# Cached attention on one core: two neighbouring tokens of a page on each partition, so that a page load is 64 rows of 6 KB and 2 KB instead of 128 rows of 3 KB and 1 KB

## The reference, cut to what matters

```python
past_len = page_table.shape[1] * PAGE_SIZE          # 16 pages x 128 tokens
g = pool[page_table]                                # pages of one sequence, in order
# mixer B, stick-breaking, 6 heads x 64, k and v of a token: 2 x 6 x 64 floats = 3 KB
z = einsum('bqhd,bkhd->bhqk', q, k) * HEAD_DIM ** -0.5
after = cumsum(log_keep, reverse=True) - log_keep
a = exp(log_sigmoid(z) + after);   y = einsum('bhqk,bkhd->bqhd', a, v)
# mixer C, sparse, 6 query heads over 2 kv heads x 64, k and v of a token: 1 KB
logits = q . k  + (0 or out of reach, from the indexer's top 256);   softmax;   y = p . v
```

## Time and profile before

| | |
|---|---|
| median of 3 runs | 4626.3 us (4622.88 to 4626.41) |
| the profiled execution | 4624.24 us, span 4622.5 us |
| mean granted TensorE clock | 0.97 |
| busy share of the span | PE 92%, PEld 52%, DVE 75%, ACT 38%, POOL 23% |
| cached attention, layer 0 | from the first page load of its own at 1833.2 us to the issue of the output stage's first load at 2053.6 us |
| cached attention, layer 1 | from 4139.8 us to 4360.4 us |

### The profile page before, as it was taken

One profiled execution on the slowest core, in us unless ns is written; L12 is line 12 of the kernel. 1 busy time (PEld: TensorE's weight loads), 2 busy tenths in 40 slices (PEclk: granted clock), 3 DMA queues, 4 the chain that ended last, 5 costly groups with the idle time before them and its releaser, 6 DMA issues.

```text
span 4622.5 us, 80699 instructions
## 1 busy us (share of the span) xinstructions
PE 4268.6 (92%) x30222; PEld 2418.8 (52%) x30222; DVE 3454.6 (75%) x5645; ACT 1737.0 (38%) x2538; POOL 1041.1 (23%) x1395
## 2 busy tenths in 40 slices
PE   8987999999999998879999879999999999987799
PEld 6433545754466676444464335457544666754443
DVE  2685999999799764554536859999997997645445
ACT  3553212211177786330035522112111777854300
POOL 4220035500033342110043100354000433411100
PEclk9998999999999999899999989999999999999899
DMA  2102210211232003884211022102112320048832
GB/s 79 32 15 62 66 24 29 77 53 51 77 112 78 27 29 126 286 276 155 93 48 31 17 64 63 24 31 77 51 53 75 116 74 27 29 135 287 276 114 91
DMA packets 344791, 397.06 MB, mean 86 GB/s; under 512 B 101335, under 2 KB 265266, under 8 KB 341074
## 3 DMA queue, kind: packets, MB, share of 16 engines
q1 hardware_dynamic: 319058, 375.11, 25.9%
q10 hardware_dynamic: 25344, 16.79, 1.3%
HBM read 297.72 MB, written 94.15 MB: 85 GB/s over the span
## 4 chain that ended last, share of the span: by engine, by line
PE 78%; issue 6%; ACT 5%; DVE 4%; DMA 3%; SPq 2%; ACTq 1%; POOL 1%; DVEq 0%; POOLq 0%
PE banks L885 20%; PE banks L888 13%; PE banks L2136 10%; PE banks L329 5%; PE banks L369 4%; PE banks L1530 3%; PE banks L1500 3%; PE banks L1212 3%; PE banks L1250 3%; PE banks L1514 2%; PE banks L1234 2%; DVE arena L1363 2%; PE banks L1833 2%; PE banks L1828 2%; PE banks L1844 1%
## 5 line engine op out<-in xcount | busy, mean ns | idle before, releaser
L1038 DVE TENSOR_SCALAR_CACHE_REDUCE arena<-arena 128x1920 uint8<-128x1920 f32 (+13 forms) x896 | 1259.1, 1474 | 0.0
L885 PE MATMUL banks<-arena 128*128 128x512 f32 x2176 | 937.4, 592 | 0.0
L885 PEld LDWEIGHTS banks<-arena 128*128 128x128 f32 x2176 | 409.9, 189 | 520.5 <-issue 520.2
L888 PE MATMUL banks<-arena 128*128 128x384 f32 (+1 forms) x2048 | 620.0, 459 | 2.4 <-POOLq L143 2.4
L1363 DVE TENSOR_TENSOR_SCAN arena<-arena 128x129 f32<-128x129 f32 (+3 forms) x480 | 535.5, 1176 | 26.7 <-ACT arena L1274 15.6
L468 DVE SCALAR_TENSOR_TENSOR arena<-arena 128x512 f32<-128x512 f32 (+3 forms) x532 | 403.7, 759 | 122.0 <-ACT arena L434 72.4
L888 PEld LDWEIGHTS banks<-arena 128*128 128x128 f32 x2048 | 380.1, 189 | 207.3 <-POOLq L143 2.6
L2136 PE MATMUL banks<-arena 128*128 128x512 f32 x1024 | 445.0, 597 | 19.1 <-DMA arena<-in_w_out 19.1
L1595 DVE CUSTOM_DVE_ANT_0 arena<-banks,arena 128x512 f32<-128x512 f32 (+3 forms) x480 | 269.4, 607 | 160.0 <-PE banks L1500 159.5
L434 ACT ACTIVATE arena<-banks 128x1024 f32<-128x1024 f32 (+3 forms) x304 | 278.5, 920 | 245.3 <-PE banks L369 139.6
L369 PE MATMUL banks<-arena 64*128 64x512 f32 (+3 forms) x1216 | 310.0, 597 | 60.5 <-ACT arena L434 59.1
(11 more groups left out here) (202 smaller groups left out, 5622.8 us busy)
## 6 DMA issues: line engine op xcount, KB each, us to landing
arena<-in_cache_sb_kv SPq DMA_DIRECT2D x256, 384.0 KB, 4.2
arena<-in_cache_dsa_kv SPq DMA_DIRECT2D x144, 128.0 KB, 4.2
arena<-in_x_prompt SPq DMA_DIRECT2D x32, 512.0 KB, 4.4
arena<-mixT SPq DMA_DIRECT2D x32, 512.0 KB, 4.0
arena<-xs SPq DMA_DIRECT2D x32, 512.0 KB, 4.4
arena<-in_cache_dsa_kv ACTq DMA_DIRECT2D x112, 128.0 KB, 4.6
arena<-in_w_in SPq DMA_DIRECT2D x8, 1536.0 KB, 7.4
out<-arena SPq DMA_DIRECT2D x64, 192.0 KB, 1.9
```

The lines of the kernel that those rows point to most:

```text
L885: m = nc.tensor.matmul(bank[i % 4][:, :], W2[c % 2][:, k, j * P:(j + 1) * P], xT[:, k, t * FREE:(t + 1) * FREE], start=(k == 0), stop=(k = ...
L888: m = nc.tensor.matmul(bank[i % 4][:, 0:WD[name]], xT[:, k, t * P:(t + 1) * P], W2[c % 2][:, k, 0:WD[name]], start=(k == 0), stop=(k == KC ...
L1038: nc.vector.tensor_scalar(dummy[j % 2][:, 0:v.shape[-1]], v, thr[:, t:t + 1], 0.0, ALU.is_ge, ALU.add, accum_out=history[:, k, t:t + 1]).t ...
```

## The change

A page now fills half of the partitions and two slots. Page jj of a chunk goes to partitions 0 to 63 (jj even) or 64 to 127 (jj odd), to slots 0 and 1 (jj < 2) or 2 and 3, and partition p of that half holds tokens 2p and 2p + 1. These two lie side by side in DRAM, and the two slots lie side by side in the buffer, so one row of a load is 6 KB (stick) or 2 KB (sparse), and a load has 64 rows. The number of loads, their bytes, their order and their queues stay. Since a slot now holds every second token of two pages, `keys` writes each transpose of 64 tokens to every second column of a PSUM bank (step of 2 floats), the two copies to `akT` read and write runs of 128 instead of 64, and `weights` reads every second column of the weights as its stationary operand.

```diff
         def by_token(keysT):
-            return keysT.rearrange("p (n e t) -> p e n t", e=2, t=HD)
+            return keysT.rearrange("p (n e t) -> p e n t", e=2, t=P)
         def halves(banks):
-            return banks.rearrange("p (e n t) -> p e n t", e=2, t=HD)
+            return banks.rearrange("p (e n t) -> p e n t", e=2, t=P)
+        def page_at(chunk_rows, jj):
+            e, k = jj % 2 * HD, jj // 2 * 2
+            return chunk_rows[e:e + HD, k:k + 2, :]
+        def tokens_of(jj):
+            first = jj // 2 * 2 * P + jj % 2
+            return slice(first, first + 2 * P - 1, 2)
         def load_stick_page(queue, l, q, jj, pg):
-            queue.dma_start(asb[q % NASB][:, jj, :], sb_pool[l, ds(pg, 1), :, :].rearrange("o p c -> (o p) c")).then_inc(s_apg[q % NASB], 16)
+            queue.dma_start(page_at(asb[q % NASB], jj), sb_pool[l, ds(pg, 1), :, :].rearrange("o (p t) c -> (o p) t c", t=2)).then_inc(s_apg[q % NASB], 16)
         def load_sparse_page(queue, l, q, jj, pg):
-            queue.dma_start(ada[q % NADA][:, jj, :], dsa_pool[l, ds(pg, 1), :, :].rearrange("o p c -> (o p) c")).then_inc(s_apg[q % NASB], 16)
+            queue.dma_start(page_at(ada[q % NADA], jj), dsa_pool[l, ds(pg, 1), :, :].rearrange("o (p t) c -> (o p) t c", t=2)).then_inc(s_apg[q % NASB], 16)
...
-                        o = (p % 2 * APC + jj) * HD
+                        o = p % 2 * FREE // 2 + jj // 2 * P + jj % 2
...
-                            k = nc.tensor.transpose(bank[p // 2 * 2 + e][:, o:o + HD], src[r, :], ident[r, r])
+                            k = nc.tensor.transpose(bank[p // 2 * 2 + e][:, o:o + P - 1:2], src[r, :], ident[r, r])
...
-                            k = nc.tensor.transpose(bank[6][:, a + jj * DROWS:a + (jj + 1) * DROWS], alg[r % 2][0:DROWS, e:e + P], ident[0:DROWS, 0:DROWS])
+                            k = nc.tensor.transpose(bank[6][:, a + jj * DROWS:a + (jj + 1) * DROWS], alg[r % 2][0:DROWS, lo:hi][:, tokens_of(jj)], ident[0:DROWS, 0:DROWS])
...
-                            k = nc.tensor.transpose(bank[6][:, jj * SROWS:(jj + 1) * SROWS], awv[m % 2][0:SROWS, jj * P:(jj + 1) * P], ident[0:SROWS, 0:SROWS])
+                            k = nc.tensor.transpose(bank[6][:, jj * SROWS:(jj + 1) * SROWS], awv[m % 2][0:SROWS, tokens_of(jj)], ident[0:SROWS, 0:SROWS])
```

More of the change, by code:

```diff
@@ L1855, in weights @@
                         for jj in range(APC):
-                            e = keys_at(c)[0] + jj * P
-                            k = nc.tensor.transpose(bank[6][:, a + jj * DROWS:a + (jj + 1) * DROWS], alg[r % 2][0:DROWS, e:e + P], ident[0:DROWS, 0:DROWS])
+                            lo, hi = keys_at(c)
+                            k = nc.tensor.transpose(bank[6][:, a + jj * DROWS:a + (jj + 1) * DROWS], alg[r % 2][0:DROWS, lo:hi][:, tokens_of(jj)], ident[0:DROWS, 0:DROWS])
                     else:
```

## The result

The changed kernel takes **4754.6 us** (4742.6 to 4758.4, 4 runs); the kernel before took 4624.9 us (4622.9 to 4626.4, 4 runs) beside it. The ratio is 1.0276, 95% interval [1.0257, 1.0296]: **slower**, by 130 us where 180 were forecast. The profiled execution took 4742.6 us, the fastest of the four, with a span of 4740.9, 118 us more than before.

What follows compares the result with a forecast made beforehand. PE's steps were taken to set the cached attention stage, with loads just in time. Loads at 205 GB/s would add 90 us per layer, 180 in all, to 4624.2: 4804 profiled, 4806 us median, range 4715 to 4875.

Steps and rivals of the forecast that it cites:

- Rows per load: Cached attention's page loads: touching 64 partitions instead of 128 gives about half the rate, as w_out's 64-row loads (203 to 214 GB/s).
- The rate: Cached attention stage: 205 GB/s, the same before and after the first ten chunks, so 62.2 MB take 303 us.
- the 5 us of slack: Last chunk's transposes started 5 us after its landing and would now start on landing.
- The second estimate of the prediction: From the Trainium skill's port rule for partitions 0 to 63: 208 GB/s and about 4798 us.
- the forecast case: Loads at about half rate bound the cached attention: 4806 us, own range 4740 to 4876, 75 in 100.
- PE and SP keep up: Per chunk of 10.2 us, PE's step takes at most 8.4 us and SP's issues 6.5, 0.18 us more per load.
- Writes to every second PSUM column: Key transposes: from below nothing, from above 24 us per layer; costed at nothing inside PE's idle time.
- The stationary operands: Weights read with step 2: at most 0.5 us per chunk, 16 us per layer; costed at nothing inside PE's idle time.
- The pages loaded ahead: 16 pages loaded during the sparse stage need 41 us at 205 GB/s, covered by 40 us of that stage: no cost.
- Halves make up for each other and longer rows pay: Rival for the page loads: full rate returns and only load waits of 7.1 + 6.4 us go, about 4611; 7 in 100.
- The rate recovers in part: Rival for the page loads: 230 to 290 GB/s, stage end moves 57 to 1 us per layer, 4740 to 4630; 10 in 100.
- TensorE becomes the cost: Rival: loads at full rate, but PSUM writes and step-2 operands cost 2 x 40 us, 4704; 5 in 100.

Runs made afterwards that it cites:

- e3: Kernel before with only the changed loads (64 rows, halves in turn), its own TensorE side kept: 4745.7 us, ratio 1.0247.
- e5: Changed kernel with all page loads on SP's queue: 4773.2 us, ratio 1.0324.
- e6: Changed kernel with lower-half pages loaded from SP's queue and upper-half pages from ScalarE's: 4785.7 us, ratio 1.0347.
- e9: Changed kernel plus two DRAM-to-DRAM copies of 8 rows per layer, meant to offset the DMA engines: 4750.9 us, ratio 1.0262.
- e2: Changed kernel with the loads of the kernel before (128 rows), changed TensorE side kept: 4629.2 us, ratio 1.0003.
- e7: Kernel with stick pages on every fourth partition, four tokens each, sparse pages as before, GpSimd writing weights in slot order: 4630.8 us, ratio 1.0011.
- e10: e3 with each page's 64 rows on every second partition instead of 64 neighbouring ones: 4632.6 us, ratio 1.0013 against the kernel before.
- e1: Loads alone, nine forms of stick pages: 128 rows 402 GB/s, halves in turn 227, lower half 206, partitions 32 to 95 421, halves by queue 277.
- e4: Loads alone, both caches in chunks: old form some 390 GB/s, halves on one queue 222, changed kernel's queues 224 to 232, queue per half 292.
- e8: Loads alone, three long streams in halves: bare 229 GB/s, with 48-row loads between 216, behind a copy of 8 rows 231, all flat.

## Why the prediction was right, and where its sizes were off

**Rows per load: right, and the only cost clear of noise.** Every variant with loads in one half was 2.5% to 3.5% slower (e3, e5, e6, e9, the changed kernel), every one that spreads them is within 0.2% of before (e2, e7, e10). The DMA share of 1.0 at about half the rate, read from `w_out` in the earlier trace rows, is what the pages show.

The Trainium skill's page "SBUF — State Buffer" ("Door 1: The DMA port swizzle") has the cause as ports: partitions 0 to 63 reach half of them. e1 agrees in kind, 206 GB/s for the lower half against 421 for partitions 32 to 95. That it is ports, no run here shows; that it is the place of the partitions, e1 and e10 do.

**The rate, the mis-sized term.** I took 205 GB/s, flat, and wrote that the rate should be the same before and after the first ten chunks. It was 214 and 216 in the first 100 us of layer 0 and 259 later, 236 over the whole; layer 1 had 215 to 229. The loads took 264 us from first issue to last landing, not 303. With the measured rates the prediction's own sum comes out: 62.2 MB / 236 GB/s is 264 us, 56 more than 208, less the 5 us of slack makes 51, and the stage grew by 50.7; for layer 1 the rate from 4190 to 4470 is 223, which gives 279 us, 73 more than 206, less 5 makes 68, and the stage grew by 66.2. So the mechanism held and this one term was off: 51 and 66 us in place of 90 each. The second estimate of the prediction, 208 GB/s and 4798 us, missed the same way. The time lies near the low edge of the forecast case's own range (4740 to 4876), and there is some luck in it: with layer 0's rate in both layers the sum would be 4624 + 102 = 4726 us (an estimate), outside that case and inside the stated range only by its reach into the partial one. Part of the error was to be seen: the 205 came from stretches of 10 and 8 us in which residual rows were mixed in, and halves in turn run at 222 to 232 by themselves (e1, e4), a rate at which I had put the forecast's own upper edge (230). Of the climb to 259, more below.

**PE and SP keep up: right.** PE is busy 195 of 264 us. It was busy 165 in the earlier trace rows; the granted clock fell from 0.89 to 0.82 and the weights' transposes are dearer, so more of the longer stage is filled by its own work, and its waits for pages came to 42.1 and 43.3 us and not to over 80. An issue took 469 ns where the earlier trace rows had 0.34, so 0.13 us more and not 0.18. One line's instructions in the changed kernel, shortest, median and longest in ns:

```profile
L1713 SPq DMA_DIRECT2D arena<-in_cache_sb_kv x256: 468/469/998, 1745.7 to 4454.7; - x128
```

**Writes to every second PSUM column: nothing, for a better reason.** I hid up to 24 us per layer behind idle time, and there was nothing to hide. The stationary operands did cost what was set as their bound. A step in the changed kernel, against the earlier trace rows:

```profile
2001.02 1.22 PE L1854 MATMUL banks<-ident,arena 64*128 64x64 f32 x32 [1.84 <-DMA arena<-in_cache_dsa_kv]
2002.08 0.63 PE L1867 MATMUL banks<-ident,arena 48*128 48x48 f32 x4
2002.63 0.79 PE L1876 MATMUL banks<-ident,arena 80*128 80x80 f32 x4
```

The 32 transposes take 1.22 us, as before. The four with a stationary operand of step 2 take 0.63 and 0.79 us for 0.40 and 0.49: 0.53 us per chunk where I had set 0.5 as the upper bound, a part of it from a clock below full (granted 0.84 in that stretch); in e2, whose loads are fast, the same rows read 0.63 and 0.70, so 0.44. e2's time shows that nearly all of it is hidden even without the idle time that I had counted on.

**The pages loaded ahead: right in the cover, wrong in the price.** They landed at about 208 GB/s, well before the stage. Yet the sparse stage of layer 0 took 108.4 us between its two stores (L1473) instead of 103.9. In that time the changed kernel's PE shows waits for its own sequencer that the kernel before doesn't have there:

```profile
1776.06 0.60 PE L1514 MATMUL banks<-ident,arena 64*128 64x64 f32 x13 [1.38 <-issue]
...
1786.83 0.66 PE L1530 MATMUL banks<-arena 128*64 128x128 f32 x7 [1.84 <-issue]
```

The two waits are 3.2 of the 4.5 us. Behind the second the granted clock was 0.96 from 1787 to 1832, where it had been 1.00, and eight matmuls of L1500 took 3.46 us for 1.94. The waits stand in the time of the saturated loads; e3, e5, e6 and e9 have the long stage too (108.9 to 109.4 us), e2, e7 and e10 don't (103.9). Layer 1 doesn't bear it out: its sparse stage stayed at 103.9 in the changed kernel, and it took 107.1 us in e10 and 107.0 in e7, whose loads are fast. That instructions are fetched late beside saturated loads is my reading, argued and not shown.

**The rivals.** "Halves make up for each other and longer rows pay" was wrong twice. The rate didn't come back, and with the rate back its gain of 13.5 us didn't come: e7 took 4.5 us of the waits for loads away and e10 3.4, and both are at 1.001. In layer 0 of both, other waits took up what was freed. That the whole 13.5 us were slack of this kind is likely but not shown, since no run removed them all. "The rate recovers in part" is where layer 0 landed (236 GB/s is in its 230 to 290), and layer 1 did not (223); the measured 4754.6 lies nearer to its 4740 than to my 4806. "TensorE becomes the cost" fell with e2.

**Open:** why the rate climbs within a stage. It isn't tied to a layer: e3, with the same loads, goes from 212 to 235 GB/s in layer 0 and from 217 to 253 in layer 1, the other way round than the changed kernel. It isn't the second queue (e5 climbs too), nor loads of 48 rows between the pages (e8, flat), and no stream of halves in turn rose above 232 where nothing else ran (e1, e4, e8). An offset between the engines was not tested cleanly.

## What to carry to other kernels

Before changing the shape of a load, list which partitions each row goes to: loads that each stayed in partitions 0 to 63 or 64 to 127 had about half the rate here, while 64 or 32 rows spread over every second or fourth partition had all of it, and alternating halves from one queue bought back a tenth. If a neighbouring stage already has a load of the new shape, its rate is a good forecast; here the short sample with other traffic in it got the sign right and the size too large. And a wait of a few microseconds on a load, in a stage whose engines work in step, need not be a gain to be had: take it away in one experiment before counting on it. A wait that gets shorter is no proof of a faster load either; look at when the load landed.

## What was not expected of the hardware

- Partitions 32 to 95 take 421 GB/s, 0 to 63 take 206 (e1). It isn't that only 64 partitions are written.
- Opposite halves from two queues that are both kept full give 277 (rows of 6 KB alone, e1) to 292 GB/s (e4), from one queue in turn 220 to 231.
- An fp32 stationary operand read with step 2 loads in 217 ns instead of 140 (80 partitions x 128, median, in e2 as in the changed kernel), while a transpose's result written to every second PSUM column costs nothing. The Trainium skill's "SBUF — State Buffer" says in its note on cachelines that non-contiguous PSUM access slows matmuls significantly; here the 2048 transposes have a median of 225 ns against 223. One line in the changed kernel, shortest, median and longest in ns, then the weight loads of the other:

```profile
L1854 PE MATMUL banks<-ident,arena x2048: 220/225/369, 1837.1 to 4471.2; 64*128 64x64 f32 x187
...
L1876 PEld LDWEIGHTS banks<-ident,arena x256: 192/217/231, 1856.1 to 4481.3; 80*128 80x128 f32 x128
```

- An issue of 64 rows costs SP more than one of 128 (469 ns against 338), whether the partitions are neighbours or every second one (475 ns, e10).
